# Sums of a forgetting gate that every partition needs: two ways to spread them in a two-layer kernel

## The reference, cut to what matters

```python
# second block, token_mixer: 8 forgetting heads of width 64
f_logit = proj[..., o:o + FOX_HEADS].astype(jnp.float32) + b_f
cum = jnp.cumsum(jax.nn.log_sigmoid(f_logit), axis=1)        # (B, T, 8)
cum_k = jnp.transpose(cum, (0, 2, 1))
...
sf = jnp.einsum('bqhd,bkhd->bhqk', qf, fk) * (FOX_HEAD_DIM ** -0.5)
sf = sf + jnp.transpose(cq, (0, 2, 1))[..., :, None] - cum_k[..., None, :]
pf = jax.nn.softmax(jnp.where(causal, sf, NEG), axis=-1)
of = jnp.einsum('bhqk,bkhd->bqhd', pf, fv)
```

## Time and profile before

| | us |
|---|---|
| median of 3 runs | 1170.4 (1168.33 to 1172.17) |
| the profiled execution | 1167.35 |
| its span, first to last instruction | 1165.3 |
| TensorE busy in it | 1130.1 |
| VectorE, ScalarE, GpSimd busy | 565.6, 567.3, 461.2 |

### The profile page before, as it was taken

How to read it: one execution, slowest core, us unless ns; L and a number is a source line. 1 busy time by engine, 2 the same in 40 slices (tenths; PEclk the granted TensorE clock), 3 DMA queues, 4 the chain that set the end, 5 groups by cost and what they waited for, 6 DMA issues and landing times.

```text
span 1165.3 us, 15160 instructions
## 1 busy us (share of the span) xinstructions
PE 1130.1 (97%) x5831; PEld 899.3 (77%) x5831; DVE 565.6 (49%) x1140; ACT 567.3 (49%) x1044; POOL 461.2 (40%) x251
## 2 busy tenths in 40 slices
PE   5999999999999999989999999998999999999997
PEld 5777878878778888878677766677888888888885
DVE  4628879778485224063344545527311112644544
ACT  5546766667768752343354545544422234333332
POOL 4153343442542444552232313325444445544441
PEclk9999999999999999999999999999999999999999
DMA  8132122221221332622222212212233333332211
GB/s 243 44 100 55 39 71 55 73 55 37 74 72 37 99 101 91 226 63 59 55 55 55 73 55 73 71 57 73 73 100 99 91 107 109 110 108 91 91 55 72
DMA packets 139801, 95.15 MB, mean 82 GB/s; under 512 B 8801, under 2 KB 124874, under 8 KB 139730
## 3 DMA queue, kind: packets, MB, share of 16 engines
q1 hardware_dynamic: 136112, 88.98, 26.2%
q10 hardware_dynamic: 3618, 5.22, 1.4%
HBM read 91.29 MB, written 2.88 MB: 81 GB/s over the span
## 4 chain that ended last, share of the span: by engine, by line
PE 91%; DVE 4%; ACT 2%; POOL 2%; issue 1%; DMA 1%; SPq 0%; DVEq 0%; ACTq 0%
PE bank L412 29%; PE bank L1157 13%; PE bank L1139 13%; PE bank L441 5%; PE bank L811 4%; PE bank L820 4%; PE bank L836 2%; PE bank L1170 2%; PE bank L920 1%; PE bank L629 1%; PE bank L957 1%; PE bank L973 1%; PE bank L647 1%; PE bank L448 1%; PE bank L427 1%
## 5 line engine op out<-in xcount | busy, mean ns | idle before, releaser
L2405 POOL TENSOR_TENSOR ring<-raw_ring,ring 128x1024 fp32r<-128x1024 f32 x159 | 393.0, 2477 | 592.4 <-ACT ring L1183 592.4
L412 PE MATMUL bank<-hT,ring 128*128 128x512 f32 x1536 | 401.2, 405 | 1.2 <-POOL ring L2405 1.2
L412 PEld LDWEIGHTS bank<-hT,ring 128*128 128x128 f32 x1536 | 277.4, 189 | 67.6 <-issue 15.0
L1183 ACT CAST ring<-raw_ring 128x1024 fp32r<-128x1024 f32 x160 | 167.3, 1047 | 110.8 <-PE bank L1157 86.8
L1157 PE MATMUL bank<-ring,ring_u 128*128 128x512 f32 x672 | 154.0, 391 | 0.0
L1139 PE MATMUL bank<-hT,ring 128*128 128x512 f32 x672 | 152.5, 389 | 0.0
L1157 PEld LDWEIGHTS bank<-ring,ring_u 128*128 128x128 f32 x672 | 126.2, 188 | 27.6
L1139 PEld LDWEIGHTS bank<-hT,ring 128*128 128x128 f32 x672 | 126.1, 188 | 26.1
L2382 DVE TENSOR_TENSOR ring_u<-u,ring_u 128x1024 fp32r<-128x1024 f32 x32 | 80.0, 2506 | 76.1 <-ACT ring_u L1755 76.1
L2387 DVE TENSOR_TENSOR u<-u 128x512 f32<-128x512 f32 x32 | 22.9, 715 | 139.2 <-ACT u L1762 139.2
L1762 ACT ACTIVATE u<-bank 128x512 f32<-128x512 f32 x32 | 19.1, 598 | 115.2 <-PE bank L1139 108.3
(11 more groups left out here) (294 smaller groups left out, 1583.4 us busy)
## 6 DMA issues: line engine op xcount, KB each, us to landing
raw_ring<-in_w_in SPq DMA_DIRECT2D x144, 256.0 KB, 3.3
raw_ring<-in_w_up SPq DMA_DIRECT2D x64, 256.0 KB, 3.2
raw_ring<-in_w_down SPq DMA_DIRECT2D x64, 256.0 KB, 2.8
raw_ring<-in_w_out SPq DMA_DIRECT2D x32, 256.0 KB, 2.9
x<-in_x SPq DMA_DIRECT2D x4, 512.0 KB, 5.6
raw_ring<-in_w_branch_sb SPq DMA_DIRECT2D x8, 256.0 KB, 2.9
raw_ring<-in_w_branch_gdn SPq DMA_DIRECT2D x8, 256.0 KB, 3.3
x<-in_x ACTq DMA_DIRECT2D x4, 512.0 KB, 5.7
```

The lines of the kernel that those rows point to most:

```text
L412: p = pe.matmul(bank, m.slab_k8(n % 4)[:, a, k, :], m.hT[:, b, k, :], start=term == 0, stop=term == 23)
L1183: act.copy(m.ring[:, q, 0, :], m.raw_ring[:, q, :]).then_inc(s.slab_hi[q], 1)
L2405: pool.tensor_tensor(m.ring[:, q, 1, :], m.raw_ring[:, q, :], m.ring[:, q, 0, :].bitcast(F32), ALU.subtract).then_inc(s.slab_lo[q], 1)
```

## The change

The sums go through HBM. VectorE writes `cumT` with the sign turned; SP stores it to a tensor `cums` in HBM and loads two rows of it for each pass, repeated on all 128 partitions (4 KB on each, 512 KB in all), into `cum`, which has two slots. `fox_max` reads `cum` in place of the copied bank and waits for the load. `pick`, its load, the eight products of `fox_decay` and their eight copies are gone, and so is the wait of `fox_z` for them; it waits for `fox_v` instead, which frees bank 6. In addition the orders of TensorE, ScalarE and VectorE are written out anew, in the second mixer and, with small shifts, in the first block too.

```diff
-        self.pick = take("pick", [8, 8 * P])
+        self.cum = take("cum", [P, 4, T])
...
+    def sums_for(i):
+        if i == 0:
+            sp.wait_ge(s.cum_out, 16)
+        if i > 1:
+            sp.wait_ge(s.f_dve[0], 16 * (i - 2) + 13)
+            sp.wait_ge(s.f_dve[1], 16 * (i - 2) + 13)
+        sp.dma_start(m.cum[:, 2 * (i % 2):2 * (i % 2) + 2, :], m.cums[2 * i:2 * i + 2, :].partition_broadcast(P)).then_inc(s.f_c[i % 2], 16)
...
         tall(SLABS_B + n, w2, w2, B_COLS[c] + i * P, 4)
+        if n == 10:
+            sp.wait_ge(s.small_dve, 31)
+            sp.dma_start(m.cums, m.cumT).then_inc(s.cum_out, 16)
+        if n == 11:
+            sums_for(0)
+            sums_for(1)
+        if n == 20:
+            sums_for(2)
...
+        if n == 2:
+            sums_for(3)
...
-    tiles.to(143)
+    tiles.to(132)
     pe.wait_ge(s.small_dve, 30)
...
-    def fox_decay(i, h):
-        pe.wait_ge(s.f_v, i + 1)
-        pe.wait_ge(s.small_dve, 31)
-        pe.matmul(banks[6 + h], m.pick[:, (2 * i + h) * P:(2 * i + h + 1) * P], m.cumT, start=True, stop=True).then_inc(s.f_cps[h], 1)
-
     def fox_z(i, t_):
...
         else:
-            pe.wait_ge(s.f_c[0], i + 1)
-            pe.wait_ge(s.f_c[1], i + 1)
+            pe.wait_ge(s.f_v, i + 1)
...
-        tiles.to(136)
         fox_rows_T(i, 1, 3)
+        tiles.to(132)
+        fox_av(i, 3)
+        tiles.to(134)
+        diff_mix(i, 4)
         tiles.rest()
-        diff_mix(i, 4)
-        fox_av(i, 3)
...
-    def fox_decay(i, h):
-        act.wait_ge(s.f_cps[h], i + 1)
-        act.copy(fox_rows[2 * h + 1], banks[6 + h]).then_inc(s.f_c[h], 1)
...
-        delta_out_high(i)
+        exponential(bv, s.v_dve, 2 * i + 3, s.v_sig)
         delta_k_square(i + 1)
...
-    dve.tensor_copy(m.cumT, banks[7][0:8, :]).then_inc(s.small_dve, 1)
+    dve.tensor_scalar(m.cumT, banks[7][0:8, :], -1.0, None, ALU.mult).then_inc(s.small_dve, 1)
...
         if t_ == 0:
-            dve.wait_ge(s.f_c[h], i + 1)
+            dve.wait_ge(s.f_c[i % 2], 16 * (i // 2 + 1))
```

More of the change, by code:

```diff
@@ L86, in bias_constants @@
     hot = (bucket(np.maximum(255 - m, 0))[None, :] == np.arange(32)[:, None]).astype(np.float32)
[L87 to L90, removed]
+    return hot
 class Memory:
@@ L206, in __init__ @@
         self.sg_bc = take("sg_bc", [P, P])
-        self.bbuf = [take(f"b{n}", [P, T]) for n in range(16)]
+        self.bbuf = [take(f"b{n}", [P, T]) for n in range(14)]
         self.post2 = at("post2", r4 + 32 * KB, [P, D])
@@ L978, in tensor_program @@
         tiles = Tall(SLABS_B + 6 * (i + 1), 6, tile_b_free(6 * (i + 1)))
-        tiles.to(5)
+        tiles.to(8)
         fox_v_rows(i)
         diff_v_rows(i, pairs)
-        tiles.to(14)
-        fox_decay(i, 1)
-        tiles.to(16)
-        fox_decay(i, 0)
-        tiles.to(20)
+        tiles.to(21)
+        diff_z_pair(i, 0, 0, pairs)
+        fox_z(i, 0)
+        tiles.to(33)
         diff_z_pair(i, 1, 0, pairs)
-        fox_z(i, 0)
-        tiles.to(23)
-        diff_z_pair(i, 0, 0, pairs)
-        tiles.to(44)
+        tiles.to(37)
+        fox_rows_T(i, 1, 0)
+        tiles.to(40)
         fox_rows_T(i, 0, 0)
-        tiles.to(53)
+        tiles.to(46)
+        fox_av(i, 0)
+        tiles.to(51)
+        fox_z(i, 1)
         diff_rows_T(i, 0, 0, pairs)
@@ L1065, in tensor_program @@
     diff_v_rows(i, last_pairs)
-    tiles.to(2)
-    fox_decay(i, 0)
+    tiles.to(6)
     diff_z(i, 0, 0, 0, last_pairs)
-    fox_decay(i, 1)
-    tiles.to(4)
+    tiles.to(8)
+    fox_z(i, 0)
+    tiles.to(9)
     diff_z(i, 1, 0, 0, last_pairs)
     diff_z(i, 0, 0, 1, last_pairs)
-    fox_z(i, 0)
-    tiles.to(9)
+    tiles.to(14)
     diff_z(i, 1, 0, 1, last_pairs)
+    tiles.to(19)
+    fox_rows_T(i, 1, 0)
     tiles.to(20)
     fox_rows_T(i, 0, 0)
-    fox_rows_T(i, 1, 0)
-    tiles.to(31)
+    tiles.to(24)
+    fox_av(i, 0)
+    tiles.to(29)
+    fox_z(i, 1)
+    tiles.to(30)
     diff_rows_T(i, 0, 0, last_pairs)
+    tiles.to(39)
     diff_rows_T(i, 1, 0, last_pairs)
-    tiles.to(33)
-    fox_av(i, 0)
-    tiles.to(34)
-    diff_av(i, 1, 0, last_pairs)
-    fox_z(i, 1)
-    tiles.to(45)
+    tiles.to(40)
     fox_rows_T(i, 0, 1)
@@ L1644, in fox_p @@
         act.wait_ge(s.f_ps[h], 12 * i + 3 * t_ + 2)
-        act.copy(fox_rows[2 * h][:, 0:w], banks[6 + h][:, 0:w]).then_inc(s.f_act[h], 1)
+        act.copy(fox_rows[h][:, 0:w], banks[6 + h][:, 0:w]).then_inc(s.f_act[h], 1)
     def fox_mix(i):
@@ L2088, in vector_program @@
     stick_gate(i)
+    delta_zero(i, 6)
     delta_level(i, 5)
-    delta_zero(i, 6)
     merge_least(5)
-    times(gate, m.rawg, gate, s.g_sig, 4 * i + 4, s.g_dve)
     stick_soft(i, 2)
@@ L2096, in vector_program @@
     delta_u(i)
+    times(qg, qT, misc, s.decay_exp, 3 * i + 2, s.qg)
     delta_state(i, 0)
@@ L2100, in vector_program @@
     merge_least(7)
+    times(gate, m.rawg, gate, s.g_sig, 4 * i + 4, s.g_dve)
     delta_state(i, 2)
@@ L2326, in vector_program @@
     diff_max(i, 0, 0, 0, 4)
+    fox_max(i, 1, 0)
+    fox_max(i, 0, 0)
     diff_max(i, 1, 0, 0, 5)
-    fox_max(i, 1, 0)
+    fox_recip(i, 0, 0)
+    fox_normed(i, 0, 0)
+    fox_recip(i, 1, 0)
     diff_max(i, 0, 0, 1, 4)
-    fox_max(i, 0, 0)
-    fox_recip(i, 1, 0)
+    fox_normed(i, 1, 0)
     diff_max(i, 1, 0, 1, 5)
-    fox_recip(i, 0, 0)
-    fox_normed(i, 1, 0)
-    fox_normed(i, 0, 0)
     diff_weights(i, 0, 0)
+    fox_o(i, 0)
     diff_weights(i, 1, 0)
-    fox_o(i, 0)
     fox_max(i, 0, 1)
```

392 lines of the change are left out of this document (189 added, 203 removed).

## The result

| | before | after |
|---|---|---|
| median of the runs compared, us | 1169.5 (1168.33 to 1172.17, 4 runs) | 1154.3 (1153.50 to 1155.46, 4 runs) |
| ratio of the two | | 0.9868, 95% interval 0.9847 to 0.9888 |
| profiled execution, us | 1167.35 | 1154.68 |
| its span, us | 1165.3 | 1153.4 |

The two profiled executions differ by 12.7 us only.

The account below looks back on a forecast made before the run. TensorE, busy 1130.1 of 1165.3 us, was taken to bound the kernel. Terms -8.4 - 1.5 - 1.6 + 0 + 1.0 + 0.6 = -9.9 us took the median 1170.4 to 1160.5, range 1154.5 to 1167.0.

Parts of the forecast that it names:

- 1, the selecting products: Eight products of line 945, 1.05 us each, leave TensorE, six in passes 0 to 2, two in the last: 8.4 us gained.
- 2, the end of pass 2: TensorE's 2.1 us wait for VectorE before the output projection shrinks, ten terms covering the mixing: 1.5 us gained, 0 to 2.1.
- 3, the lowered clock: Of two clock falls, 678 to 682 and 732 to 736, one vanishes: 1.6 us gained, between 0 and 3.1.
- The footing: Profiled execution lay 3.05 us below the median of the runs, so the forecast was put on the median, 1170.4.
- 4, the transfer: Store and loads of the sums arrive before the first `fox_max` or at most 1.8 us late: cost 0, at most 1.1.
- the slack of 0.7: Time left for TensorE at the first `fox_rows_T`: 4.6 us of cover against about 3.9 from first maximum to scaled weights.
- the bounds of 3.8 and 7.5 for the load: Time for the repeated 512 KB load, taken from the two loads of `post`, landing between 567.5 and 571.2.
- 5, less cover: Last pass, 72 products for cover: waits of 0.5 to 0.8 at blocks 2 and 3; 1.0 us lost, 0 to 2.1.
- 6, the orders elsewhere: Moved orders outside the second mixer's main changes, seven passes at -0.3 to +0.6 each: +0.6 us, bounds -1 and +4.
- That both falls stay or turn up elsewhere: Rival: clock falls follow where such work lies in time, so no clock gain, 1162.1 us; chance 0.20.
- That the cover gives out: Rival: TensorE waits instead of computing, about 5 of the 9.9 us given back, 1165.5; in part, chance 0.18.
- VectorE held behind GpSimd: Rival: GpSimd splits stretch two-operand VectorE work in seven passes, 1.9 us each, 13.3 lost, 1173.8; slower, chance 0.06.

Follow-up runs that it names:

- mech_old_orders: Kernel before with only the HBM transfer, selecting products and their copies gone, every other instruction in its old place: 1157.3 us, ratio 0.9882.
- before_wide: Kernel before with its eight selecting products on 128 rows instead of 8, fed a constant pattern, so scores lack their gate: 1162.6 us, ratio 0.9939.
- late_load: Changed kernel with the first two loads of sums issued one slab later in SP's queue: 1163.2 us.
- old_first_block: Changed kernel with the orders of the kernel before, on all engines, in the whole first block: 1154.2 us, ratio 0.9862.
- idle_products_8: Changed kernel plus eight unused products on 8 rows, two ahead of the first forgetting scores of each pass: 1167.9 us.
- filled_waits: Changed kernel plus three unused 128x512 products in each TensorE wait ahead of the turned rows after a residual: 1153.1 us, repeated 1153.4 us.

## Why the prediction was right and wrong, point by point

**1, the selecting products (8.4): right.** mech_old_orders is 8.9 us shorter at full clock, 1.1 a product; the passes of 53.06 became 50.85, and two products put back cost 2.1 us again.

**2, the end of pass 2 (1.5): the wait right in size, not in its reason.** It went from 2.07 to 0.72, by 1.35. The mixing has time; what is left is a copy of the last tile by ScalarE, which the forecast did not look for.

**3, the lowered clock (1.6, bounds 0 to 3.1): the step that failed.** The clock gave 6.5. Two things were wrong in the term. It expected only one of the two falls to go, and both went: 3.4 us in the profiled executions instead of 1.6. And it took the two falls of one profiled execution, 3.1 us, as the upper bound of what the clock can give; the ordinary runs gave 3 us more than the falls that the profiles show. Over the whole span the three profiled executions of the kernel before lost 8.2, 8.2 and 10.5 us and its 46 runs 12.7 on average, so they were mild ones; the changed kernel's three lost 4.6, 6.9 and 6.9, and its 13 runs 6.2. That the extra loss comes with the narrow products too, before_wide shows: wide products in the same places give back 5.9 us of clock. In which stretches it lies stays open.

On the cause: before_wide shows that with wide products both falls vanish even with the wait in place, and mech_old_orders that without any product a fall at the wait stays. So narrow products and a wait can each bring a fall; the changed kernel has no such products and 0.7 us of the wait.

The footing is the same mistake seen from the other side. The profiled execution lay 3.05 us below the median, and the text carried that gap over to the kernel after as if it were the same for both. It was clock: the kernel after shows 1154.68 profiled against 1155.4 in the median. Of the miss of 5.3, 4.9 are in this term (6.5 for 1.6), the rest in the others together.

**4, the transfer (0): right, and narrowly.** `cumT` is ready at 562.8 (forecast 561.5, with the terms before it 1.3 us later than in the profile of before), the loads are issued 2.7 us later (2.2 forecast), and no maximum waits. late_load shows how little room is left; the slack of 0.7 was on the careful side (1.1 there; from the first maximum to the end of the first scaled weights it took 2.9 us in the changed kernel and not 3.9), and the bounds of 3.8 and 7.5 for the load hold (5.0 to 7.3 for the first pair, from kernel to kernel).

**5, less cover (+1.0): not as waits.** In the last stretch TensorE waits 44.93 - 43.86 = 1.1 us, and 48.35 - 47.17 = 1.2 before. The places named (blocks 2 and 3) have waits of 0.6 and 0.4, but they took the place of others as long.

**6, the orders elsewhere (+0.6, -1 to +4): none in the first block.** old_first_block equals the changed kernel, and the waits at L569 are what they were at L551.

**Items 2, 5 and 6 together** were forecast at +0.1 us, and the changed kernel equals mech_old_orders at full clock (1147.4 and 1147.3). That they agree is partly luck: the 1.35 us of item 2 came back in another way than 5 and 6 had it, as 0.3 us more in a pass with TensorE busy all the time (50.86 for 50.55). Item 1 put the changes between terms and small products at nothing; whether it is these, no run separates.

**The rivals.** That both falls stay or turn up elsewhere (1162.1) is refuted: the four stretches show 1.00, and no profiled execution of the changed kernel loses clock between 520 and 786. The sentence beside it took from the Trainium skill (TensorE: Matmul & The Clock Gate, Part 1) that the clock follows how busy the engine has been, and concluded that a fall without idle time would stay. It went. In idle_products_8 the clock goes to 0.50 with TensorE busy in all of every stretch, behind the products on 8 rows only, so idle time is not the only thing that takes it down here. That idling does it too, late_load and filled_waits show. That the cover gives out did not happen, and VectorE held behind GpSimd cost nothing: the operation of the earlier trace rows (L2227 after) takes 353 ns at most, not 2494.

At full clock the forecast was -8.4 - 1.5 + 1.0 + 0.6 = -8.3, and the runs show -8.8.

## What to carry to other kernels

Read the granted clock of a stretch beside its length, and split each run's time into span times clock and the rest before you explain a difference; a lowered clock that one profile shows is a sample, not a bound. In this kernel eight products on 8 rows cost TensorE their length (7.7 us) and then again most of that in clock (5.7), so moving rows of numbers to all partitions by DMA paid, with the store issued 9.4 us ahead of the first use. Work out for such a load the time from issue to landing (5.0 to 7.3 us here for the first 512 KB), and what TensorE loses beyond the wait if it is late: here 8 us for a wait of 6.1.

## What the runs showed of the hardware

- TensorE's clock fell to 0.50 with the engine busy throughout, behind products on 8 rows (idle_products_8, 626 to 628), and not behind products as long on 128 rows. Eight of them cost 5.7 us of clock, sixteen 12.7; the operands' values differed between the kinds too.
- The same program's mean clock varies from run to run, 0.985 to 0.993 over 46 runs of the kernel before, and its time with it, 1174.6 to 1166.5 us. The changed kernel's 13 runs keep to 0.993 to 0.996 and 1153.3 to 1156.5.
- Two products of 512 columns on different halves of the rows took 1.02 us, on all rows 1.98.
- A single product on 8 rows between terms on 128 cost 0.2 to 0.4 us more at full clock than one on 128 rows (before against before_wide, 1.6 us for eight, 0.8 in a pass of two); two in a row cost the same on 8 and 128 rows (passes of 52.95 and 52.97).
- Behind a store of 16 KB to HBM the dependent load was issued 2.7 us later, with the load of a slab between them (1.5 us in mech_old_orders); the first two loads of 512 KB, repeated over the partitions, landed 5.7 us after their issue in one kernel and 7.2 in another, the later ones 4.5 to 5.1.
